# A threshold search by bits in a hybrid decoder layer: the whole search ahead of retention, with ScalarE counting the last block by signs

## The reference, cut to what matters

```python
h = rms_norm(x, pre_mix_g[i]);  proj = h @ w_in[i]
r_q, r_k, r_v, r_g, a_q, a_c, i_q, i_k, i_w = split_cols(proj)
...                                  # rotation; chunkwise retention -> y_ret
# dsa_sparse_attention, for each block of 128 rows t:
rel = relu(einsum('bthd,bsd->bths', qi_b, ki))
iscore = einsum('bths,bth->bts', rel, wi_b)          # indexer scores, f32
iscore = where(s_idx <= t, iscore, -inf)
_, sel = lax.top_k(iscore, 256)                      # ties: the lower index first
...                                  # softmax over the 256 chosen, latent values
mix = concatenate([y_ret, y_dsa]) @ w_out[i];  x = x + rms_norm(mix, ...)
...                                  # SwiGLU FFN, gated per-layer embedding
```

## Time and profile before

| | us |
|---|---|
| median of 3 runs | 1430.89 (1429.82 to 1433.61) |
| span of the profiled execution | 1428.3 |
| TensorE busy | 1376.4 |
| VectorE busy | 1013.1 |
| ScalarE busy | 605.1 |
| GpSimd busy | 329.0 |
| projection ends, retention begins | 331.9 |
| attention | 460 to 680 |
| FFN | 680 to 1300 |

### The profile page before, as it was taken

The page is one execution under the profiler, slowest core; times in us unless marked ns, Lnnn a source line. Parts: engine busy times, 40 slices in busy tenths (PEclk is TensorE's granted clock), DMA queues, the critical chain, the costliest instruction groups (busy, mean ns, idle before and its releaser), DMA issues.

```text
span 1428.3 us, 19391 instructions
## 1 busy us (share of the span) xinstructions
PE 1376.4 (96%) x7142; PEld 1125.8 (79%) x7142; DVE 1013.1 (71%) x1592; ACT 605.1 (42%) x1229; POOL 329.0 (23%) x383
## 2 busy tenths in 40 slices
PE   7999999999989889998999999999999999999998
PEld 7887888887777567777778888888887888888886
DVE  5748789998999546765877777777776765565633
ACT  6434552315823776574522222222222656453221
POOL 4545457711541475652000000000000000000000
PEclk9999999999999999999999999999999999999999
DMA  6322223225323021133234555444458866662211
GB/s 215 82 56 71 79 84 116 94 92 192 111 101 143 31 74 61 45 91 107 55 131 165 177 177 177 161 148 153 156 193 289 316 239 223 237 213 75 67 53 45
DMA packets 137150, 189.02 MB, mean 132 GB/s; under 512 B 12768, under 2 KB 75616, under 8 KB 137056
## 3 DMA queue, kind: packets, MB, share of 16 engines
q1 hardware_dynamic: 120224, 152.17, 32.5%
q10 hardware_dynamic: 16832, 35.61, 6.5%
HBM read 130.08 MB, written 57.67 MB: 131 GB/s over the span
## 4 chain that ended last, share of the span: by engine, by line
PE 79%; DVE 7%; issue 4%; ACT 4%; POOL 3%; DMA 1%; DVEq 1%; SPq 0%; ACTq 0%; POOLq 0%
PE ps L728 23%; PE ps L729 23%; PE ps L730 23%; PE ps L930 2%; PE ps L922 2%; PE ps L941 1%; PE ps L769 1%; POOL mxs L2721 1%; DMA raw<-in_w_in 1%; DVE sc L1915 1%; ACT lm L1444 1%; DVEq L1931 1%; PE ps L857 1%; PE ps L892 1%; PE ps L855 1%
## 5 line engine op out<-in xcount | busy, mean ns | idle before, releaser
L2593 POOL TENSOR_TENSOR smf<-smf,sml 128x1 f32<-128x1 f32 x16 | 9.1, 579 | 739.3 <-DVE smf L2474 625.2
L728 PE MATMUL ps<-bh,ah 128*128 128x512 f32 x308 | 120.1, 390 | 2.4 <-DVE u2b L2315 2.4
L730 PE MATMUL ps<-bh,al 128*128 128x512 f32 x308 | 119.9, 389 | 0.0
L729 PE MATMUL ps<-bl,ah 128*128 128x512 f32 x308 | 119.8, 389 | 0.0
L728 PE MATMUL ps<-wbh,xth 128*128 128x512 f32 (+1 forms) x320 | 118.9, 371 | 0.0
L729 PE MATMUL ps<-wbl,xth 128*128 128x512 f32 (+1 forms) x320 | 117.7, 368 | 0.0
L730 PE MATMUL ps<-wbh,xtl 128*128 128x512 f32 (+1 forms) x320 | 117.7, 368 | 0.0
L2421 DVE TENSOR_TENSOR al<-ra,ah 128x512 fp32r<-128x512 f32 x77 | 53.1, 690 | 70.7 <-ACT ah L1671 70.3
L728 PE MATMUL ps<-th,ssh 128*128 128x512 f32 x240 | 93.6, 390 | 1.8 <-DVE u2b L2291 1.2
L730 PE MATMUL ps<-th,ssl 128*128 128x512 f32 x240 | 93.4, 389 | 0.0
L729 PE MATMUL ps<-tl,ssh 128*128 128x512 f32 x240 | 93.4, 389 | 0.0
(11 more groups left out here) (375 smaller groups left out, 3871.1 us busy)
## 6 DMA issues: line engine op xcount, KB each, us to landing
raw<-in_w_in SPq DMA_DIRECT2D x49, 256.0 KB, 3.0
wt<-in_w_ffn_down SPq DMA_DIRECT2D x44, 256.0 KB, 7.2
down_sums<-wt ACTq DMA_DIRECT2D x44, 256.0 KB, 5.0
ra<-hidden_sums SPq DMA_DIRECT2D x44, 256.0 KB, 2.9
rb<-down_sums SPq DMA_DIRECT2D x44, 256.0 KB, 3.5
raws<-in_w_ffn_gate SPq DMA_DIRECT2D x21, 512.0 KB, 3.9
raws<-in_w_ffn_up SPq DMA_DIRECT2D x21, 512.0 KB, 5.3
ret_rows<-stg SPq DMA_DIRECT2D x32, 320.0 KB, 3.4
```

What stands on the lines that cost most here:

```text
L728: pe.matmul(o, ah, wh, start=start, stop=False, skip_group_check=resumes)
L729: pe.matmul(o, ah, wl, start=False, stop=False, skip_group_check=resumes)
L730: return pe.matmul(o, al, wh, start=False, stop=stop, skip_group_check=resumes)
```

## The change

It has five parts. FLIP moves from SBUF to the last columns of PSUM bank 7, and with it the junk of block 4's count goes from PSUM to SBUF. Behind A's 32 bits, VectorE takes B's sign step over three blocks, and then 31 bits in which it counts blocks 5 and 6 only. ScalarE counts block 7 (`count_by_scalar`): the signs of candidate minus score, summed up by the accumulator, over 1024 columns, with the other result thrown into pair 2 of PSUM; two such counts stand behind each evacuation of units 39 to 54, the last alone. `set_bit` takes block 7's flip from that sum by a comparison of its own, after a wait for ScalarE (a_cnt), and ScalarE waits for each candidate (v_cand). A sign of 0 counts for half, so that block 7's threshold can come out just below the 256th score: `next_above` mends this once. A's six tie pieces stand behind bits 4, 8, 12, 16, 20 and 24 of B, and B's nine pieces behind its last bit, all of it ahead of the retention's first instruction on VectorE. TensorE's `pair_bank(0)` waits for the 32nd candidate in addition, since the retention's scores use pair 2. Two pairs of semaphores are merged into one each (a_sq and a_sqs, p_wr and p_rs).

```diff
-    FLIP = sb("flip", [P, RT - B0], 1.65625, I32)
+    FLIP = PS[:, 8 * 512 - 8:8 * 512 - 8 + RT - B0].bitcast(I32)
...
-    BITS_AHEAD, BITS_BETWEEN, BITS_MIX = 20, 3, 9
-    PIECES_AT = {13: 1, 21: 1, 29: 1, 37: 2, 45: 2, 53: 2}
+    BY_SCALAR = RT - 1
+    BITS_BY_SCALAR = SIGN
+    SCALAR_FROM, SCALAR_PER = 39, 2
+    TIES_BETWEEN = {4: (B0 + 1, 0), 8: (B0 + 1, 1), 12: (B0 + 1, 2), 16: (B0 + 2, 0), 20: (B0 + 2, 1), 24: (B0 + 2, 2)}
...
                 pe.wait_ge(s["v_mask"], 3)
+                pe.wait_ge(s["v_cand"], SIGN + 1)
                 keep_clock(6, 6)
...
+        def count_by_scalar(n):
+            act.wait_ge(s["v_cand"], n + 1)
+            i = BY_SCALAR - B0
+            sc.activation(pair(2), SC[i][:, :], ACT.Sign, scale=-1.0, bias=CAND[:, i:i + 1].bitcast(F32),
+                          accum_out=CNT[:, i:i + 1]).then_inc(s["a_cnt"], 1)
...
             evacuate(g)
+            for n in scalar_bits(g):
+                count_by_scalar(n)
...
+        def search_with_scalar(m):
+            for b in SEARCH_B:
+                if b != BY_SCALAR:
+                    ins = count(b, bound(b), ALU.is_ge, JUNKB[b][:, :])
+            link(ins)
+            set_bit(SEARCH_B, m)
...
+                j, q = slice(blocks[0] - B0, BY_SCALAR - B0), slice(BY_SCALAR - B0, BY_SCALAR - B0 + 1)
+                v.tensor_scalar(FLIP[:, j], CNT[:, j], float(TOPK), float(1 << m), ALU.is_lt, ALU.mult)
+                dve.wait_ge(s["a_cnt"], SIGN - m)
+                link(v.tensor_scalar(FLIP[:, q], CNT[:, q], float(HALF_COUNT), float(1 << m), ALU.is_gt, ALU.mult))
...
+        def next_above(b, junk):
+            i = slice(b - B0, b - B0 + 1)
+            r, inc, size = bound(b), STEP[:, 0:1], STEP[:, 1:2]
+            link(count(b, r, ALU.is_gt, junk))
+            v.tensor_scalar(inc, CNT[:, i], float(TOPK), ULP, ALU.is_ge, ALU.mult)
+            link(v.tensor_scalar(size.bitcast(I32), CAND[:, i], (1 << SIGN) - 1, None, ALU.bitwise_and))
+            link(v.scalar_tensor_tensor(r, size, inc, r, ALU.mult, ALU.add))
...
-        for b in SEARCH_A:
-            count_ties(b, TIE_A, count_junk(b))
-            rank_ties(b, TIE_A, RANK_A)
-            found_mask(b, RANK_A)
         dve.wait_ge(s["p_caus"], RT - B0)
-        for m in range(SIGN, SIGN - BITS_AHEAD, -1):
-            search_step(SEARCH_B, m, JUNKB)
+        search_step(SEARCH_B, SIGN)
+        for m in range(SIGN - 1, -1, -1):
+            search_with_scalar(m)
+            if SIGN - m in TIES_BETWEEN:
+                tie_piece(*TIES_BETWEEN[SIGN - m])
+        next_above(BY_SCALAR, JUNKB[BY_SCALAR][:, :])
+        for b in SEARCH_B:
+            for part in range(3):
+                tie_piece(b, part)
...
             ret_center(hp)
-            search_step(SEARCH_B, SIGN - BITS_AHEAD - hp, JUNKM)
...
         query_parts(0)
-        for m in range(BITS_MIX - 1, -1, -1):
-            search_step(SEARCH_B, m, JUNKM)
...
-            for _ in range(PIECES_AT.get(t, 0)):
-                search_piece(pieces)
-                pieces += 1
```

More of the change, by code:

```diff
@@ L103, in build @@
     CAND = sb("cand", [P, RT - B0], 1.625, I32)
-    FLIP = sb("flip", [P, RT - B0], 1.65625, I32)
+    STEP = sb("step", [P, 2], 1.65625)
     CNT = sb("cnt", [P, RT - B0], 1.6875)
@@ L141, in build @@
     JUNK3 = sb("junk3", [P, (B0 + 2) * P], 206.5, mybir.dt.uint8)
+    JUNK4 = sb("junk4", [P, (B0 + 3) * P], 172, mybir.dt.uint8)
     JUNKB = {b: sb(f"junkb{b}", [P, (b + 1) * P], 164 + (b - B0 - 3) * 1.25, mybir.dt.uint8) for b in range(B0 + 3, RT)}
[L143 to L148, removed]
+    TIE, RANK = (sb(n, [P, S], a, mybir.dt.bfloat16) for n, a in (("tie", 168), ("rank", 170)))
     STG = [sb(f"stg{i}", [P, RW], 200.5 + 2.5 * i) for i in range(2)]
@@ L326, in build, with scalar_bits @@
     SIGN = 31
-    BITS_AHEAD, BITS_BETWEEN, BITS_MIX = 20, 3, 9
-    PIECES = 3 * len(SEARCH_B)
-    PIECES_AT = {13: 1, 21: 1, 29: 1, 37: 2, 45: 2, 53: 2}
-    assert sum(PIECES_AT.values()) == PIECES
+    BY_SCALAR = RT - 1
+    BITS_BY_SCALAR = SIGN
+    SCALAR_FROM, SCALAR_PER = 39, 2
+    def scalar_bits(g):
+        first = (g - SCALAR_FROM) * SCALAR_PER
+        return range(max(0, first), min(BITS_BY_SCALAR, first + SCALAR_PER)) if g >= SCALAR_FROM else range(0)
+    TIES_BETWEEN = {4: (B0 + 1, 0), 8: (B0 + 1, 1), 12: (B0 + 1, 2), 16: (B0 + 2, 0), 20: (B0 + 2, 1), 24: (B0 + 2, 2)}
     HALF = (slice(0, HD), slice(HD, P))
@@ L417, in build @@
                [("fo1", r) for r in range(4)] + [("u", i) for i in range(RT + 1)])
-    sq_at = {u: n + 1 for n, u in enumerate(squares)}
+    sq_at = {u: RT + n + 1 for n, u in enumerate(squares)}
     PROLOGUE = ((0, 0), (1, 0), (0, 1), (1, 1))
@@ L1263, in square @@
             if r:
[L1264 to L1265 removed]
+                act.wait_ge(s["a_sqs"], r)
+            sc.activation(pair(3), XN[r][:, :], ACT.Square, accum_out=cols["ss0"][:, r:r + 1]).then_inc(s["a_sqs"], 1)
         def x_hi(r):
@@ L1942, in bound, with search_step @@
             return CAND[:, b - B0:b - B0 + 1].bitcast(F32)
-        def count_junk(b):
-            return JUNK3[:, :] if b == B0 + 1 else pair(3, (b + 1) * P)
-        def search_step(blocks, m, junks=None):
+        def search_step(blocks, m):
             for b in blocks:
-                ins = count(b, 0.0 if m == SIGN else bound(b), ALU.is_ge, junks[b][:, :] if junks else count_junk(b))
+                ins = count(b, 0.0 if m == SIGN else bound(b), ALU.is_ge,
+                            (JUNK3, JUNK4)[b - B0 - 1][:, :] if blocks is SEARCH_A else JUNKB[b][:, :])
             link(ins)
             set_bit(blocks, m)
+        def search_with_scalar(m):
[4 more added lines that the diff above has]
+            set_bit(SEARCH_B, m)
         def set_bit(blocks, m):
@@ L1980, in found_mask, with tie_piece @@
             v.tensor_scalar(sc_b, sc_b, MASKED, None, ALU.mult).then_inc(s["v_mask"], 1)
-        def search_piece(p):
-            b, part = SEARCH_B[p // 3], p % 3
-            tie, rank, junk = (TIE_B, RANK_B, JUNKT) if p < 3 else (TIE_C, RANK_C, JUNKC)
-            if p == 3:
-                dve.wait_ge(s["v_qlo"], KT + NP)
+        def tie_piece(b, part):
+            junk = (JUNK3, JUNK4)[b - B0 - 1] if b in SEARCH_A else JUNKB[b]
             if part == 0:
-                count_ties(b, tie, junk[:, 0:(b + 1) * P])
+                count_ties(b, TIE, junk[:, :])
             elif part == 1:
-                rank_ties(b, tie, rank)
+                rank_ties(b, TIE, RANK)
             else:
-                found_mask(b, rank)
+                found_mask(b, RANK)
         early = [(B0, n) for n in range(ROUNDS_B0)]
@@ L2320, in row_half @@
             ins.then_inc(s["v_ht"], 1)
-        pieces = 0
         for t in range(STEPS + TAIL):
```

37 lines of the change are left out of this document (22 added, 15 removed).

## The result

The changed kernel takes 1438.05 us (median of 4 runs, 1437.18 to 1438.90) against 1430.94 in the runs of the kernel before made beside it: a ratio of 1.0049, 95% interval 1.0036 to 1.0062. It is slower by 7.1 us. The forecast was 1439. The profiled execution spans 1435.5 us against 1428.3.

What follows compares the result with a forecast made beforehand. TensorE, busy 96%, was taken to bound the kernel. 10.7 + 0.5 - 1 - 1.5 = +8.7 us on the span of 1428.3; the difference added to the median 1430.89 gave 1439.6, forecast 1439 us, range 1435 to 1445.

Steps and rivals of the forecast that it cites:

- A's tail: SEARCH_A's last 21 steps on VectorE: 2.03 us each with FLIP in PSUM, ending at 245.7, 12.7 earlier.
- Rival A: SEARCH_A's small operations: PSUM frees nothing, A ends at 258.45, time 1452; chance 0.12.
- The bits: SEARCH_B's 31 bits after the sign step: 2.65 us each, nearer the linked (2.72) than the unlinked bound (2.52); 82.2 us.
- Rival C: VectorE-ScalarE hand-over: late counts or semaphore waits cost 8 to 10 us, retention starts at 351, time 1448; chance 0.09.
- A's ties: Block A's tie pieces between SEARCH_B's bits on VectorE: 11 us in the chain, bounds 10 and 13.
- the gate: TensorE's wait for the 32nd candidate at the retention's start: 342.6 in place of 331.88, +10.7 us.
- Where TensorE loses it: TensorE before the retention: most of the time lost in projection units from 39 on, little at the end.
- The sign that I had named: Projection units on TensorE: spaced 6 us from unit 40.
- Behind the gate: VectorE after the 32nd candidate: some 23 us of count and ties, just covered by 23.1; a 5 us late centring absorbed.
- Given back: Time saved after the retention's start: 1 us in the retention, 0 in the mix, 1.5 in the attention.
- Rival B: Freed VectorE helps GpSimd; TensorE's waits from 332 to 680 fall 5 to 8 us, time 1430 to 1433; chance 0.13.
- the 0.5 of contention: VectorE's ties beside GpSimd's selects early in the retention: 0 to 2 us added, 0.5 in the sum.

Runs made afterwards that it cites:

- both experiments on FLIP: Kernel before with only SEARCH_A's FLIP in PSUM and block 4's junk in SBUF: 1431.03 us; changed kernel with FLIP back in SBUF: 1455.93 us.

## Why the prediction was right

**A's tail.** Forecast 245.7, measured 245.18: the steps are 1.98 us, the lower bound, since the read of the accumulator behind the count whose junk went from PSUM to SBUF is shorter as well (0.08 us against 0.14). Rival A fell with the means of 164 and 157 ns. The rule of the Trainium skill, "SBUF — State Buffer", section "Who interferes with whom", that one of two instructions which need the shared port waits for the whole of the other, is borne out by both experiments on FLIP: the held-up comparison shown above ends at 265.49, GpSimd's instruction at 265.46. The one of "VectorE: DVE Perf Modes" in the Trainium skill, section "The TRN2 errata", by which a PSUM source has 120 fixed cycles where SBUF has 58, is not: the operation with CAND in SBUF and FLIP in PSUM took 157 ns, the same with both in SBUF and undisturbed 0.16 us. For operations this small the measurement decides.

**The bits.** Forecast 2.65, measured 2.58: 31 x 0.07 is 2.2 of the 2.4 us by which the 32nd candidate (340.15) came ahead of the 342.6; the first candidate, 0.7 early, and the ties, 0.5 late, nearly cancel. The wait on ScalarE, because of which I had stayed near the linked end, isn't there; L1982 costs 0.07. Rival C fell: VectorE waited for ScalarE nowhere, and a count with its read takes 1.24 us from start to end, against 1.3.

**A's ties.** Forecast 11, measured 11.5: the one term of the gate that was sized too small.

**Where TensorE loses it.** I wrote "most of the time in the units, little at the end". The projection's last matmul starts at 337.27 in place of 331.64, 5.6 later (0.5 of it from the start of the program), and then TensorE waits 2.6. That is two thirds and a third, so the second half of my sentence was too strong. The sign that I had named is there: the evacuations of units 40 to 47 stand 6.0 us apart on average (252.95 to 295.01) in place of 5.44.

**Behind the gate.** Forecast 23 us of VectorE's work in 23.1, measured 23.2 to the first centring, with no wait before it and none caused. This was right by a hair, and its second sentence was wrong: I held that a centring up to 5 us late would be taken up by the steps that leave the retention. With the centring 6.9 late, as with A's ties behind the bits, 6.9 us were lost up to the last y. A centring 5 late was not run. The error had no part in the time, since the case did not arise.

**Given back.** Forecast 1 in the retention and 1.5 in the attention. The retention gave 0.2 (82.6 against 82.8), and not by the steps that left it: the 0.2 are there before the first centring, at TensorE's first wait in the retention (12.9 us after the start against 13.1). TensorE's wait of 0.6 for a select, which I thought might go, stands unchanged. The attention gave 1.4 (6.3 to 4.9). That is 1.6, of which 1.2 arrive at the end of the program; where the other 0.4 went is open. Rival B needed more than 7 and fell.

The sum: 8.4 at the gate (10.7 forecast), 1.2 given back (2.0 with the 0.5 of contention set against it). Both were sized too large, and since they have opposite signs a part of the error cancelled: 8.7 became 7.2. That part is luck, and so are the 0.5 of the 8.4 that were there before the search and are not the change's. The path, the wait at the gate and its place are as forecast.

## What to carry to other kernels

Work that no one waits for is free only where it stands: moving it ahead of a stage makes its whole chain count, and here the 83.5 us of SEARCH_B's sign step and bits with 11.5 us of A's ties had room for the bits alone. Before a search, a sort or a mask is pulled forward, lay its chain against the end of the stage that covers it, and move out of the chain whatever does not feed the next step; with the ties in the mix the same code lost its 8.5 us. A late operation costs by who is queued behind its waiter, so look at the in-order queue of the engine that waits for it.

## What the runs showed of the hardware

Two elements per partition took 650 ns on average in SBUF beside a busy GpSimd, and 164 ns with the result in PSUM: the place of a tiny tile can be worth more than the operation. With FLIP in SBUF the hold-up did not come evenly. In the search of SEARCH_B one of two comparisons took 1.0 us and the next 0.17, as a GpSimd instruction was running or not. GpSimd is held up in turn: a causal select on GpSimd that takes 0.41 us alone took 1.02 beside a scan of the ties in the changed kernel (at 359.14), and 1.40 beside another in the version with A's ties in the retention (at 341.63). And waits of the same length did not have the same clock behind them: after the wait of 2.6 us in the changed kernel six transposes took 0.85 us (granted clock 1.00 from 340 to 342 us), after one of 2.64 with FLIP in SBUF 1.51 (0.50 from 360 to 362). What sets the two apart was not tested.
